# Two-stage float32 transformer kernel: high parts kept per ring slot, low parts written in place, and weight splits made two chunks ahead

## The reference, cut to what matters

```python
h  = h  + HALF * gt1 * swiglu(ada_norm(h,  g_ffn1[l], sh1,  sc1),  w1_ffn1[l], w3_ffn1[l], w2_ffn1[l])
hc = hc + HALF * cgt1 * swiglu(ada_norm(hc, g_ffn1[l], csh1, csc1), w1_ffn1[l], w3_ffn1[l], w2_ffn1[l])
...   # conv, Fourier and latent attention branches, merged by gates, times w_out
h  = h  + HALF * gt3 * swiglu(ada_norm(h,  g_ffn2[l], sh3,  sc3),  w1_ffn2[l], w3_ffn2[l], w2_ffn2[l])
```

## Time and profile before

| what | value |
|---|---|
| median of 3 runs | 2969.06 us (2967.04 to 2971.77) |
| the profiled execution | 2967.06 us |
| its span, first to last instruction | 2965.3 us |
| PE busy | 2846.4 us, 96% |
| DVE, ACT busy | 1649.4 us (56%), 1128.8 us (38%) |
| moved from HBM | 397.4 MB, 134 GB/s over the span |
| mean granted PE clock | 0.988 of full speed |

### The profile page before, as it was taken

The page is one execution under the profiler, slowest core; times in us unless marked ns, Lnnn a source line. Parts: engine busy times, 40 slices in busy tenths (PEclk is TensorE's granted clock), DMA queues, the critical chain, the costliest instruction groups (busy, mean ns, idle before and its releaser), DMA issues.

```text
span 2965.3 us, 45314 instructions
## 1 busy us (share of the span) xinstructions
PE 2846.4 (96%) x16592; PEld 2371.2 (80%) x16592; DVE 1649.4 (56%) x2829; ACT 1128.8 (38%) x1715; POOL 49.8 (2%) x36
## 2 busy tenths in 40 slices
PE   8999999999999999999999999999999998999998
PEld 7759998669988888775666778888788887788998
DVE  6546656456666565677334466555533336645665
ACT  4345534345442222334554132221322223684443
POOL 0100001000000000030000000000000000000000
PEclk9999999999999999999999999999999999999999
DMA  5564553665544443321221234443323233234454
GB/s 193 195 224 150 179 181 129 227 222 195 175 142 147 138 147 128 120 91 45 73 70 55 89 114 148 139 136 132 101 96 99 92 94 101 84 115 149 159 179 144
DMA packets 118360, 400.11 MB, mean 135 GB/s; under 512 B 12896, under 2 KB 20960, under 8 KB 117856
## 3 DMA queue, kind: packets, MB, share of 16 engines
q1 hardware_dynamic: 115120, 391.43, 39.7%
q10 hardware_dynamic: 3120, 7.07, 0.7%
HBM read 397.40 MB, written 1.05 MB: 134 GB/s over the span
## 4 chain that ended last, share of the span: by engine, by line
PE 84%; DVE 6%; issue 3%; ACT 3%; DMA 2%; DVEq 1%; POOL 1%; SPq 0%; ACTq 0%; POOLq 0%
PE bank L814 23%; PE bank L821 22%; PE bank L824 22%; PE bank L2247 4%; PE bank L1544 2%; DVE w_lo L773 2%; DMA ring<-weights 2%; PE bank L1992 1%; PE bank L1972 1%; ACT w_hi L745 1%; PE bank L905 1%; DVE hn_lo L1025 1%; DVE work L2061 1%; PE bank L1282 1%; POOL w_lo L773 1%
## 5 line engine op out<-in xcount | busy, mean ns | idle before, releaser
L773 DVE TENSOR_TENSOR w_lo<-ring,w_hi 128x1024 fp32r<-128x1024 f32 (+1 forms) x538 | 650.2, 1209 | 842.1 <-ACT w_hi L745 839.4
L745 ACT ACTIVATE w_hi<-ring 128x1024 fp32r<-128x1024 f32 (+1 forms) x538 | 563.0, 1047 | 1349.5 <-PE bank L814 1257.0
L821 PE MATMUL bank<-hn_hi,w_hi 128*128 128x256 f32 (+1 forms) x2816 | 889.2, 335 | 0.0
L824 PE MATMUL bank<-hn_lo,w_hi 128*128 128x256 f32 (+1 forms) x2816 | 888.7, 335 | 0.0
L814 PE MATMUL bank<-hn_hi,w_lo 128*128 128x256 f32 (+1 forms) x2816 | 560.0, 341 | 24.7 <-DVE w_lo L773 20.6
L821 PEld LDWEIGHTS bank<-hn_hi,w_hi 128*128 128x128 f32 x2816 | 539.9, 192 | 52.3
L824 PEld LDWEIGHTS bank<-hn_lo,w_hi 128*128 128x128 f32 x2816 | 539.9, 192 | 52.2
L814 PEld LDWEIGHTS bank<-hn_hi,w_lo 128*128 128x128 f32 x2816 | 444.8, 191 | 95.8 <-issue 39.4
L821 PE MATMUL bank<-hid_hi,w_hi 128*128 128x512 f32 (+1 forms) x704 | 248.7, 363 | 0.0
L824 PE MATMUL bank<-hid_lo_a,w_hi 128*128 128x512 f32 (+1 forms) x640 | 226.2, 363 | 0.0
L814 PE MATMUL bank<-hid_hi,w_lo 128*128 128x512 f32 (+1 forms) x704 | 157.4, 364 | 7.9 <-DVE work L2173 4.9
(11 more groups left out here) (321 smaller groups left out, 2990.7 us busy)
## 6 DMA issues: line engine op xcount, KB each, us to landing
ring<-weights SPq DMA_DIRECT2D x692, 512.0 KB, 3.4
ring<-weights SPq DMA_DIRECT2D x32, 384.0 KB, 3.1
ring<-weights SPq DMA_DIRECT2D x32, 256.0 KB, 2.6
ring<-weights SPq DMA_DIRECT2D x28, 192.0 KB, 2.4
con<-consts ACTq DMA_DIRECT2D x1, 2063.0 KB, 7.5
con<-consts ACTq DMA_DIRECT2D x1, 1088.0 KB, 5.0
res<-ctx_cm ACTq DMA_DIRECT2D x1, 1024.0 KB, 12.5
con<-params ACTq DMA_DIRECT2D x1, 1024.0 KB, 7.5
```

The lines of the kernel that those rows point to most:

```text
L745: act.activation(w_hi[:, even, 0:w], ring[:, slot, 0:w], ACT.Copy).then_inc(s.w_hi, 1)
L773: eng.tensor_tensor(w_lo[:, even, 0:w], ring[:, slot, 0:w], w_hi[:, even, 0:w].bitcast(F32), ALU.subtract).then_inc(s.w_lo, 1)
L821: pe.matmul(dst, high, x_hi(k), start=False, stop=False)
L824: mm = pe.matmul(dst, high, x_lo(k), start=False, stop=(stop and k == order[-1]))
```

## The change

`w_hi` gets one buffer for each ring slot, and the low part is written over the weights in the ring: `w_lo[n]` is the same memory as `ring[n]`, read as fp32r. The memory needed is the same (16 KB a partition for the ring and 16 KB for the parts). `lo_used` and all waits on it are gone: a split waits for its chunk's landing alone, since the load itself waits for `used`.

```diff
+AHEAD = {"in_t": (3, 1), "up": (3, 1), "down": (2, 1), ("ffn1", 0): (2, 1), ("ffn1_out", 0): (2, 1), ("conv_in", 0): (2, 0), ("ffn2", 0): (2, 1), ("ffn2_out", 0): (2, 1),
+         ("ffn1", 1): (2, 1), ("ffn1_out", 1): (2, 1), ("conv_in", 1): (3, 0), ("ffn2", 1): (3, 1),
+         ("ffn2_out", 1): (2, 1)}
...
+        early, shift = AHEAD.get((name, l), AHEAD.get(name, (1, 0)))
...
-        ring = sb("ring", [P, SLOTS, SLOT_TILES * P])
-        w_hi = sb("w_hi", [P, 2, SLOT_TILES * P], F32R)
-        w_lo = sb("w_lo", [P, 2, SLOT_TILES * P], F32R)
+        ring_at = free[0]
+        ring = [sb(f"ring{n}", [P, SLOT_TILES * P]) for n in range(SLOTS)]
+        w_lo = [nc.alloc_sbuf_tensor_at(f"w_lo{n}", [P, SLOT_TILES * P], F32R, offset=ring_at + 4 * SLOT_TILES * P * n)
+                for n in range(SLOTS)]
+        w_hi = sb("w_hi", [P, SLOTS, SLOT_TILES * P], F32R)
...
             wait_weights(act, lin, at, c)
-            if not (isinstance(number, int) and number < 2):
-
-                act.wait_ge(s.lo_used, number)
             w = lin.tiles[c] * P
-            act.activation(w_hi[:, even, 0:w], ring[:, slot, 0:w], ACT.Copy).then_inc(s.w_hi, 1)
+            act.activation(w_hi[:, slot, 0:w], ring[slot][:, 0:w], ACT.Copy).then_inc(s.w_hi, 1)
...
-        def second_split_high(act, lin):
...
+        def early_splits(split, eng, lin):
+
+            for j in range(1, lin.early):
+                split(eng, lin, Group(0, 0, 0, period(lin.cpg)), j)
...
+        def split_ahead(split, eng, lin, g, j, following=None):
+
             n_split = len(lin.split)
...
+            j += lin.shift
+            if not isinstance(g.m, int):
+                split(eng, lin, g, j)
+                return
+            at = g.m * n_split + j - lin.n * n_split
+            if at < 0:
+                if g.m * n_split + j >= lin.early:
                     split(eng, lin, g, j)
...
+            elif following is not None and (at == 0 or at == 1 and not following.both_early and following.shift):
+                split(eng, following, Group(0, 0, 0, period(following.cpg)), at)
...
             if lin is not None:
+                early_splits(split_high, act, lin)
                 if before is not None:
                     wait_last(act, before)
-                second_split_high(act, lin)
...
             for m in range(lin.n + 1):
-                if m < lin.n:
-                    splits_ahead(split_high, act, lin, Group(m, m, 0, period(1)))
                 if m:
...
+                if m < lin.n:
+                    splits_ahead(split_high, act, lin, Group(m, m, 0, period(1)))
...
                 if g is not None:
-                    split_ahead(split_low, dve, lin, g, 1)
+                    split_ahead(split_low, dve, lin, g, 1, out)
...
                     if seqs(l) > 1:
+                        pool.wait_ge(s.w_lo, PLAN["lat_in", l].split0)
                         for g in turns(pool, PLAN["lat_in", l]):
```

More of the change, by code:

```diff
@@ L62, with __init__ @@
 class Product:
-    def __init__(self, chunk, group, n, tiles, split, split0, own):
+    def __init__(self, chunk, group, n, tiles, split, split0, own, early, shift):
+        self.early, self.shift = early, shift
         self.chunk, self.group, self.n, self.tiles, self.cpg = chunk, group, n, tiles, len(tiles)
@@ L141, in stream_plan @@
         own = {"in_a": 1, "ffn1": 2, "ffn1_out": 3, "ffn2": 2, "ffn2_out": 3}.get(name, len(tiles))
-        plan[name, l] = Product(chunk, group, n, tiles, split, split0, own)
+        early, shift = AHEAD.get((name, l), AHEAD.get(name, (1, 0)))
+        plan[name, l] = Product(chunk, group, n, tiles, split, split0, own, early, shift)
         chunk += n * len(tiles)
@@ L808, in split_product @@
             wait_split(pe, lin, g, c)
-            number = lin.split0 + g.at * len(lin.split) + lin.split.index(c)
+            slot = slot_of(lin, g, c)
             order = order or range(lin.tiles[c])
@@ L813, in split_product @@
                     wait_part(0, k)
[L814 to L818, removed]
+                pe.matmul(dst, w_lo[slot][:, k * P:(k + 1) * P], x_hi(k), start=(start and k == order[0]), stop=False)
             for k in order:
-                high = w_hi[:, number % 2, k * P:(k + 1) * P]
+                high = w_hi[:, slot, k * P:(k + 1) * P]
                 pe.matmul(dst, high, x_hi(k), start=False, stop=False)
@@ L824, in split_product @@
                 mm = pe.matmul(dst, high, x_lo(k), start=False, stop=(stop and k == order[-1]))
-            mm.then_inc(used[slot_of(lin, g, c)], 1)
+            mm.then_inc(used[slot], 1)
         def normed_hi(w):
@@ L905, in ada_pe @@
                     mm = pe.matmul(ada_bank(h)[rows, :], cs[:, k, COND_AT - 2 * q:COND_W - 2 * q],
-                                   ring[:, slot, i * 4 * P:(i + 1) * 4 * P], start=(q == 0 and k < COL_GROUPS),
+                                   ring[slot][:, i * 4 * P:(i + 1) * 4 * P], start=(q == 0 and k < COL_GROUPS),
                                    stop=(q == ADA_QUADS[h] - 1 and k >= COL_GROUPS))
@@ L1455, in first_pair @@
             wait_banks(pe, lin, at[0][0])
-            even = [(lin.split0 + c) % 2 for c in range(2)]
+            slot = [slot_of(lin, *at[c]) for c in range(2)]
             for c in range(2):
@@ L1470, in first_pair @@
                         pe.wait_ge(s.split_normed, KT * n + k + 1)
[L1471 removed]
+                    mm = pe.matmul(dst[c], w_hi[:, slot[c], k * P:(k + 1) * P], hn_lo[:, k, 0:w],
                                    start=False, stop=(k == KT - 1))
[L1473 to L1475 removed]
+                mm.then_inc(used[slot[c]], 1)
         def dense_t(pe, lin, norm):
@@ L1708, in block1_act @@
             for g, prev in turns_behind(act, lin):
-                if g is not None:
-                    splits_ahead(split_high, act, lin, g, PLAN["down", l])
                 if prev is not None:
@@ L1718, in block1_act @@
                     act.activation(tmp3[:, q, 0:T], tmp2[:, q, 0:T], ACT.Square).then_inc(s.up_v, 1)
+                if g is not None:
+                    splits_ahead(split_high, act, lin, g, PLAN["down", l])
             lin = PLAN["down", l]
@@ L2054, in gated_norm_dve @@
             w = norm_width(n)
-            second_split_low(dve, PLAN[("ffn1", "conv_in", "ffn2")[which], l])
+            early_splits(split_low, dve, PLAN[("ffn1", "conv_in", "ffn2")[which], l])
             for k in range(KT):
@@ L2626, in load @@
                         number = k * seg.pattern.count(w) + (seg.at.get(w, 0) + seg.pattern[:c].count(w))
-                        sp.dma_start(ring[:, slot, 0:w * P], streams[w][number]).then_inc(landed[slot], 16)
+                        sp.dma_start(ring[slot][:, 0:w * P], streams[w][number]).then_inc(landed[slot], 16)
                 first = per if seg.chunk < SLOTS else 0
```

62 lines of the change are left out of this document (18 added, 44 removed).

## The result

The changed kernel takes 2994.58 us (median of 4 runs, 2992.90 to 2996.01) against 2968.05 of the kernel before beside it (4 runs, 2965.77 to 2971.77): a ratio of 1.0092, 95% interval 1.0080 to 1.0104. It is slower by 26.5 us; 3002 was predicted, with a range of 2978 to 3020.

The account below looks back on a forecast made before the run. PE, busy 96% of the span, was taken as the bound. Losses of 54.5 us minus gains of 21.6 gave +33 on the profiled 2967.1: 3000, or 3002 against the median, range 2978 to 3020.

Parts of the forecast that it names:

- The loop: Layer 0's feed-forwards: DVE's work, slot release, load and high split form a closed chain, mean 11.8 us against PE's 10.88.
- A group: Layer 0's feed-forwards: PE waits about 0.9 us in each of 19 groups, 17.5 us lost per feed-forward, twice 35.
- Start: First groups of layer 0's feed-forwards, up to chunk a_2: 2.7 us lost in the first, 2.2 in the second.
- End: Before each output product of layer 0: 6.9 us of wait in place of 1.30, 5.6 more, twice 11.2.
- Clock: After the two new gaps of 7 us PE runs at a lower granted clock: 1.7 us lost each, 3.4 together.
- The gain: Waits for low parts go in input products, narrow and last feed-forwards and third products after norms: 21.6 us in sum.
- the waits of the earlier trace go because a split two ahead is early enough: Steady state: some 6 us from `used` to the low part, against three products of 5.44 us or about 2.9.
- The eviction now ahead of the split: Delays a high part by at most 0.9 us, hidden by a product of lead; otherwise the old waits return.
- The input products: Waits for low parts go: 1.2 us gained in the first input product, 2.1 in the second.
- The loop does not bind: Rival for layer 0's feed-forwards: loads or landings kinder than read, only the gains remain, 2946 us; chance 0.1.
- The loop eats only the slack: Rival for layer 0's feed-forwards: loop of 11.2 us, losses 28, 2975 us in all; chance 0.06.
- The clock falls with it: Rival for layer 0's feed-forwards: each wait lowers PE's clock, group 12.6 us, +29, 3031 us in all; chance 0.04.

Follow-up runs that it names:

- buffers-only: Changed kernel with one split ahead everywhere and high splits back ahead of evictions, keeping buffers per slot and low parts in place: 2945.43 us, ratio 0.9931.
- old order: High splits put back ahead of evictions in `in_t` and `up`: 2948.53 us from the kernel of 2947.14 us, 2936.51 us from that of 2935.17 us.
- e5_in_one: The kernel of 2947.14 us with one split ahead instead of two in the input products (`in_t`): 2935.17 us, ratio 0.9901.
- wide one ahead: Changed kernel with the second split ahead taken back in layer 0's feed-forwards and their output products alone: 2947.14 us, ratio 0.9934.

## Why the prediction was right

**The loop** was there, at the place and by the chain that was written down, and it is shown and not only argued: moving 1.2 us of DVE's work past the slot's release gave back 36 us, adding 1.3 to it cost 62, and taking the second split ahead away cost nothing and gave 47. By the steps of the sum, from the timeline of the changed kernel:

- DVE's piece 7.1 predicted, 7.10 measured. Release to low split 4.8 predicted, 4.43 in the turn shown, and a median of 4.54 and 4.61 over the first 20 turns of the two feed-forwards (4.35 to 5.09). In the turn shown the steps are

```profile
1004.34 0.92 SPq L2614 DMA_DIRECT2D ring<-weights  x2
...
1007.49 1.06 ACT L749 ACTIVATE w_hi<-ring 128x1024 fp32r<-128x1024 f32 x1 [8.23 <-DMA ring<-weights]
```

  so 0.2 from the release at 1004.16 to the load, 3.15 to ACT, 1.1 to DVE. Over those turns the load took 3.25 and 3.33 us in the median (3.06 to 3.81) where 3.4 was put in, and ACT began 0.02 us after the landing where 0.1 was put in without a row. These two small excesses are what the loop's sum had wrong: 7.10 and the medians give 11.64 and 11.71. The estimate from the page's figure, 3.2 us by the Trainium skill, "SBUF — State Buffer", section on the DMA setup-cost knee, lay about as near to these loads as the median of the earlier trace rows did.
- A group: from 895.24 to 1116.07 PE does 19 groups, 11.62 each (predicted 11.8), and in the second feed-forward, 1764.08 to 1986.85, 11.72. Over 10.88 that is 14.1 and 16.0 us where 17.5 each was predicted.
- Start: 2.34 and 2.49, predicted 2.7 and 2.2.
- End: 6.20 and 6.24 in place of 1.30 and 1.27, so 4.9 and 5.0; predicted 5.6.
- Clock: the two output products took 2.3 and 2.0 us more, predicted 1.7 each. First the stretch behind the first gap, against the earlier trace rows, then the loop with what stands before it, then its start behind the wait of 2.34 us, then the loop without its start:

```profile
1133.40:1138.20 4.80, 4.76 (x11) 3.80 (x12) 3.94 (x7) 0.00 (x0) 0.00 (x0) 0.50 0.34 113
...
885.00:1133.00 248.00, 231.98 (x995) 186.21 (x993) 139.53 (x196) 56.65 (x66) 0.00 (x0) 0.99 0.38 133
...
895.24:899.40 4.16, 4.16 (x11) 3.28 (x12) 3.95 (x6) 0.00 (x0) 0.00 (x0) 0.59 0.12 46
899.40:1131.00 231.60, 219.92 (x950) 176.74 (x949) 128.62 (x179) 52.56 (x62) 0.00 (x0) 1.00 0.39 135
```

Sum of the losses: 21.3 + 23.5 + 4.3 = 49.1, predicted 54.5; the experiment that takes the loop out gives 47.4.

**The gain** came out at the predicted size for partly the wrong reason. The kernel without the loop is 2947.14, ratio 0.9934 (0.9913 to 0.9956), which is 20 us under the kernel before, predicted 21.6. That the two agree so well is in part luck: the changed kernel gains 5.3, 9.2 and 6.0 us in the two narrow stages and the last feed-forward, where 2.2, 8.0 and 4.2 were predicted, and it loses in the input stages. And the step "the waits of the earlier trace rows go because a split two ahead is early enough" credited the second split ahead with all of it. The buffers-only kernel, which splits one ahead, has 2945.43. What went there is the wait of a high split for the product that still read the half buffer (`lo_used`): it was what held ACT in the earlier trace rows (4.38 us behind PE's bank) and in the last feed-forward's output product (44.1 us behind PE's bank, 23 times, before; 39.0 us behind landings, 22 times, with the buffers only). At the norms the second high split has moved forward as well, and which of the two took away the waits of the third products was not separated. By pieces, one ahead with buffers per slot already removes the waits of the wide third products and of the last output product (last feed-forward 197.8 against 204.5). Only the second narrow product, `down` of layer 1, needs the second split ahead (narrow stage 200.0 us; 194.0 and 195.5 with two ahead in the old order, 191.3 with evictions first): there DVE's low splits stand behind its own evictions (in the buffers-only kernel a low part whose high part is there at 803.67 begins at 804.42, behind five such operations from 802.24 on). And the parts interact, which the prediction priced at nothing: evictions first costs 26 us with one ahead, and with two ahead it gains 2 to 4 us in each narrow stage. "The eviction now ahead of the split delays a high part by at most 0.9 us, which a whole product of lead hides; if that lead is gone it comes back as the old waits" was right in its first half; the last half had no price, and the waits that came back are mostly not the old ones but new ones of 0.31 us in `up`.

**The input products** were wrong in sign: 1.2 and 2.1 us of gain were predicted, 2.4 and 0.8 of loss came. The step that failed is that of a split made ahead as having no one behind it but the norm. On ACT the evictions are queued behind it, and at the kernel's start the weights land late (ACT 4.54 us before a landing). This is shown for the first input product; the 0.8 us of the second are no more than the clock can make between two executions. Taking two ahead out of both is worth 12 us by the runs, 9.5 of it in those stages. The first input product's norm also waited 3.00 us for ACT in place of 2.2, which had been left out of the sum.

**The rivals.** "The loop does not bind" is out: the waits for the multiplication went from 4 to 38, and 32 of the new ones stand inside the two feed-forwards. "The loop eats only the slack" took a loop of 11.2; the mean groups were 11.62 and 11.72. "The clock falls with it": from 899.40 to 1131 us, with 15 waits of 0.2 to 0.9 us, the granted clock was 1.00. Those waits did not bring it down. The 0.99 of the longer stretch is mostly the fall behind the wait of 2.34 us, to 0.59 over 4.16 us; it cost nothing, as the loop and not PE sets the groups after it. Behind the wait of 2.49 us in the second feed-forward the clock stayed at 1.00. The section on HAM oscillation of the Trainium skill's "TensorE: Matmul & The Clock Gate" tells of longer waits; the gaps of 6.20 and 6.24 us, each followed by the low clock, agree with it. With one more row product, where 14 waits of 1.6 to 2.7 us stand in it, the same stretch of the changed kernel was lower:

```profile
907.00:1161.00 254.00, 226.32 (x947) 180.56 (x945) 148.51 (x214) 50.94 (x61) 0.00 (x0) 0.97 0.35 122
```

So the rival's mechanism exists, but even with those longer waits the clock fell behind some and not behind each: if each of the 14 had brought a stretch like the earlier trace rows, the mean would be 0.91.

**What stays open.** How much of the 12 us of `e5_in_one` is the clock was not separated. Nor was it tried to let a load take another slot than the row chunk's, which would break the loop at the load instead of at DVE's order. In wide one ahead the feed-forwards and their output products were taken back together, so the share of each is not known.

## What to carry to other kernels

A buffer that an engine off the critical path gives back, and for whose next content the same engine then waits in order, is a closed loop: add up that engine's work between the wait and the release, the load and whatever stands before the wait, and compare the sum with the bound engine's group before splitting further ahead. If it is longer, first move the release ahead of what can wait. And where a change has several parts, run the part that removes a wait by itself: here it had 20 us, as much as all the parts together without the loop, and one of the others cost 26 us unless a third covered it. Two orders with the same median need not be the same: compare them by stage before calling one idle.

## What was not expected of the hardware

- The granted clock took many short waits without a fall. With 15 waits of 0.2 to 0.9 us it stayed at 1.00 over 231 us; with 14 waits of 1.6 to 2.7 us it was 0.97 over 254 us; a wait of 2.34 us was followed by 0.59 over 4.16 us and one of 2.49 us by 1.00; after a gap of 6.20 us PE ran 4.8 us at 0.50, its lower level of 1.2 GHz. So a gap's length alone does not tell whether a fall follows.
- Executions of the same kernel differ in it. Those of `e5_in_one` have a mean granted clock of 0.987 to 0.991 and take 2941.74 to 2932.74 us. A thousandth is 3 us of work at the full clock, so a few us between single executions need not be the program's.
- At the start of the kernel, with constants and context being loaded beside the weights, a chunk took 6.0 us from issue to landing, and kept ACT waiting 4.54 us of it, where landings in the feed-forward took 3.1 to 4.9 us in all.
